# FFN output matrix by Strassen's scheme: 18 of 22 depth tiles, activation sums on VectorE, weight sums on GpSimd

## The reference, cut to what matters

```python
def swiglu(h, w_in, w_out):
    gate, up = jnp.split(h @ w_in, 2, axis=-1)
    return (jax.nn.silu(gate) * up) @ w_out
# per layer: D_MODEL = 1024, D_FF = 2816
x = x + 0.5 * swiglu(rms_norm(x, ffn1_norm[layer]), ffn1_w_in[layer], ffn1_w_out[layer])
x = x + mixer(rms_norm(x, mix_norm[layer]))
x = x + 0.5 * swiglu(rms_norm(x, ffn2_norm[layer]), ffn2_w_in[layer], ffn2_w_out[layer])
```

## Time and profile before

| | |
|---|---|
| median of 3 runs | 2288.98 us (2287.26 to 2289.0) |
| profiled execution, span from first to last instruction | 2285.9 us |
| median less that span | 3.1 us |
| TensorE busy | 2249.8 us (98%) |
| VectorE busy | 1633.5 us (71%) |
| ScalarE busy | 1049.8 us (46%) |
| GpSimd busy | 302.4 us (13%) |

### The profile page before, as it was taken

One profiled execution on the slowest core, in us unless ns is written; L12 is line 12 of the kernel. 1 busy time (PEld: TensorE's weight loads), 2 busy tenths in 40 slices (PEclk: granted clock), 3 DMA queues, 4 the chain that ended last, 5 costly groups with the idle time before them and its releaser, 6 DMA issues.

```text
span 2285.9 us, 45730 instructions
## 1 busy us (share of the span) xinstructions
PE 2249.8 (98%) x18915; PEld 2198.7 (96%) x18915; DVE 1633.5 (71%) x2712; ACT 1049.8 (46%) x1949; POOL 302.4 (13%) x257
## 2 busy tenths in 40 slices
PE   9999999999999999999999999999999999999998
PEld 8999999988989999999999999999988899999998
DVE  7876776557575977767877776689755657777674
ACT  5544444333323544444554444454444544444443
POOL 2100002000051100001200000144033632000001
PEclk9999999999999999999999999999999999999999
DMA  4222323322202233222222232322310012222321
GB/s 135 93 93 97 103 92 110 98 81 83 90 10 93 75 101 103 93 93 93 93 93 93 96 105 87 114 74 75 93 52 2 30 31 91 93 93 93 98 97 68
DMA packets 175052, 194.82 MB, mean 85 GB/s; under 512 B 4826, under 2 KB 155870, under 8 KB 174841
## 3 DMA queue, kind: packets, MB, share of 16 engines
q1 hardware_dynamic: 161902, 181.64, 24.3%
q10 hardware_dynamic: 12306, 8.18, 1.3%
q0 software_dynamic: 640, 2.10, 0.3%
HBM read 185.80 MB, written 6.10 MB: 84 GB/s over the span
## 4 chain that ended last, share of the span: by engine, by line
PE 85%; DVE 8%; ACT 2%; issue 2%; POOL 1%; DMA 1%; ACTq 0%; SPq 0%; DVEq 0%; POOLq 0%
PE ps L892 33%; PE ps L793 29%; PE ps L666 12%; DVE cacc L2419 2%; DVE wl L651 1%; PE ps L3320 1%; DVE pre L2408 1%; ACT cacc L2488 1%; DMA xnat<-x_prompt 1%; PE ps L1681 1%; PE ps L3165 0%; POOL dBl L2996 0%; PE ps L2152 0%; PE ps L3150 0%; PE ps L3200 0%
## 5 line engine op out<-in xcount | busy, mean ns | idle before, releaser
L892 PE MATMUL ps<-bop,wh 128*128 128x272 f32 x4032 | 761.0, 288 | 0.0
L892 PEld LDWEIGHTS ps<-bop,wh 128*128 128x128 f32 x4032 | 633.0, 188 | 0.0
L892 PE MATMUL ps<-bop,wl 128*128 128x272 f32 x2016 | 582.2, 289 | 0.0
L784 DVE TENSOR_TENSOR wl<-raw,wh 128x512 fp32r<-128x512 f32 (+1 forms) x456 | 317.5, 708 | 266.8 <-ACT wh L778 262.1
L892 PEld LDWEIGHTS ps<-bop,wl 128*128 128x128 f32 x2016 | 378.8, 188 | 0.0
L778 ACT ACTIVATE wh<-raw 128x512 fp32r<-128x512 f32 (+1 forms) x456 | 265.3, 611 | 217.2 <-PE ps L793 177.4
L793 PE MATMUL ps<-hl,wh 128*128 128x288 f32 (+1 forms) x1408 | 290.4, 287 | 0.0
L793 PE MATMUL ps<-hh,wl 128*128 128x288 f32 (+1 forms) x1408 | 289.5, 287 | 0.0
L793 PE MATMUL ps<-hh,wh 128*128 128x288 f32 (+1 forms) x1408 | 289.1, 286 | 0.0
L666 PE MATMUL ps<-xh,wh 128*128 128x288 f32 (+1 forms) x1056 | 224.7, 294 | 2.1 <-DVE wl L651 2.1
L778 ACT ACTIVATE wh<-wsum 128x512 fp32r<-128x512 f32 x256 | 159.6, 627 | 132.8 <-DVE wsum L1038 86.6
(11 more groups left out here) (490 smaller groups left out, 3586.5 us busy)
## 6 DMA issues: line engine op xcount, KB each, us to landing
raw<-ffn_w_in SPq DMA_DIRECT2D x88, 1024.0 KB, 5.0
raw<-ffn_w_out SPq DMA_DIRECT2D x32, 1024.0 KB, 5.1
raw<-odd_w_in SPq DMA_DIRECT2D x16, 1024.0 KB, 5.7
raw<-even_w_in SPq DMA_DIRECT2D x14, 1024.0 KB, 5.0
raw<-ffn_w_out SPq DMA_DIRECT2D x16, 768.0 KB, 4.2
raw<-even_w_out SPq DMA_DIRECT2D x4, 1024.0 KB, 5.0
raw<-odd_w_out SPq DMA_DIRECT2D x4, 1024.0 KB, 4.9
xnat<-x_prompt SPq DMA_DIRECT2D x2, 1024.0 KB, 11.9
```

The source lines that it names most:

```text
L784: nc.vector.tensor_tensor(lo[:, 0:nk, :], op_source(u, i), hi[:, 0:nk, :].bitcast(F32), ALU.subtract).then_inc(op_lo.sem, 1)
L892: ins = nc.tensor.matmul(ps[:, bank, 0:TH], w[:, k, :], bop[:, r, k, :], start=i in S_OPEN and k == 0 and a == 0, stop=k == KH - 1 and a = ...
```

## The change

The output matrix is multiplied by the same scheme over 18 of its 22 hidden tiles: three parts of three pairs of hidden tiles. A part has four "out" units, each with two output column tiles (256 columns) and six hidden tiles, seven blocks of 3 x 3 = 9 matmuls of 272 columns. They stand between the gate and the up unit of pairs 3, 6 and 9. The remaining four hidden tiles are multiplied plainly in two last units of four output columns each.
- The activations' blocks of a pair of hidden tiles (the two token halves of both tiles and four differences, `hidden_turns`) are made on VectorE during the unit after the pair's up unit, split by ScalarE and VectorE, and kept in `hop` (three pairs of buffers, which lie over `xh`, `xl` and the arena).
- The weight sums of all but the first two Strassen units, and those of the out units, are made by GpSimd (`block_sums_pool`).
- ScalarE copies four bank states of each out unit, at scale 0.5, into `comb`; VectorE adds them and two banks to `x` in five steps (`x_add` 1 to 4, and the fifth in `tail_dve`).

The core of the diff:

```diff
-MID_TILES = 4
-MID_PARTS = 4
+MID_PAIRS = 3
+MID_TILES = 2 * MID_PAIRS
+MID_PARTS = 3
 LAST_TILES = FT - MID_TILES * MID_PARTS
...
         for j in range(FJ):
-            for s in range(2):
-                add("whole" if j == 0 and s == 0 else "plain" if j < LEAD_PAIRS else "seven", j, s)
-            if LEAD_PAIRS <= j < LEAD_PAIRS + 2 * MID_PARTS:
-                add("mid", (j - LEAD_PAIRS) % 2, 0, (j - LEAD_PAIRS) // 2)
-        for q in range(4):
-            add("last", q, q % 2, MID_PARTS)
+            kind = "plain" if j < LEAD_PAIRS else "seven"
+            add("whole" if j == 0 else kind, j, 0)
+            if j and j % MID_PAIRS == 0:
+                for q in range(4):
+                    add("out", q, 0, j // MID_PAIRS - 1)
+            add(kind, j, 1)
+        for q in range(2):
+            add("last", q)
...
+    O_BANK = (4, 7, 4, 7, 4, 6, 4)
...
+    def early_block(u):
+        return u.block - first_block[u.f] < 2
...
-        if u.kind == "seven" and i in S_SUMS:
-            act.wait_ge(sum_made.sem, sum_made.at(4 * u.seven + S_SUMS[i] + 1))
+        if u.n_ops == 7 and i in S_SUMS:
+            sum_wait(act, u, S_SUMS[i] + 1)
...
+    def ffn_out_pe(pe, u):
+        f, p, q = u.f, u.part, u.pair
+        third = hidden_before(f, MID_PAIRS * (p + 1))
+        for i, o in enumerate(S_ORDER):
+            op = u.op + i
+            pe.wait_ge(op_lo.sem, op_lo.at(op + 1))
+            if q == 0 and i < 2:
+                pe.wait_ge(hl_ready.sem, hl_ready.at(third - (2 if i == 0 else 0)))
...
+            if i == 0 and u.out >= 2:
+                pe.wait_ge(x_part.sem, x_part.at(x_steps(u.out - 2, 5)))
+            elif i in (1, 5) and u.out >= 1:
+                pe.wait_ge(x_part.sem, x_part.at(x_steps(u.out - 1, 4)))
+            elif i in (2, 3, 4):
+                pe.wait_ge(bank_copied.sem, bank_copied.at(4 * u.block + i - 1))
+            elif i == 6:
+                pe.wait_ge(bank_copied.sem, bank_copied.at(4 * u.block + 4))
+            w_hi, w_lo = entry(op)
+            for k in range(MID_PAIRS):
+                for a, (w, r) in enumerate(((w_hi, 7 + o), (w_hi, o), (w_lo, 7 + o))):
+                    ins = nc.tensor.matmul(ps[:, block_bank(u, i), 0:TH], w[:, k, :], hop[k][:, r, :],
...
+    def hidden_turns(dve, u):
+        if not by_blocks(u):
+            return
+        f = hopf[u.pair % MID_PAIRS]
+        dve.wait_ge(h_made.sem, h_made.at(2 * FJ * u.f + 2 * u.pair + 2))
+        nc.vector.tensor_tensor(f[:, 3, :], sq[0][:, TH:T], sq[0][:, 0:TH], ALU.subtract).then_inc(turn_made.sem, 1)
+        nc.vector.tensor_tensor(f[:, 1, :], sq[1][:, TH:T], sq[0][:, TH:T], ALU.subtract).then_inc(turn_made.sem, 1)
+        dve.wait_ge(turn_made.sem, turn_made.at(turns_before(u) + 1))
+        nc.vector.tensor_tensor(f[:, 2, :], sq[1][:, TH:T], f[:, 3, :], ALU.subtract).then_inc(turn_made.sem, 1)
+        dve.wait_ge(turn_made.sem, turn_made.at(turns_before(u) + 3))
+        nc.vector.tensor_tensor(f[:, 0, :], sq[1][:, 0:TH], f[:, 2, :], ALU.subtract).then_inc(turn_made.sem, 1)
+
+    def hidden_lo(dve, u, step):
...
+            i, (at, n) = u.pair % MID_PAIRS, ((6, 1), (4, 2), (0, 4))[step]
+            src = (sq[0][:, 0:TH], two(sq[1][:]), hopf[i][:, 0:4, :])[step]
...
+    SUM_TERMS = (((1, 0), (1, 1), ALU.add), (None, (0, 0), ALU.subtract), ((0, 1), None, ALU.subtract), ((0, 0), (1, 0), ALU.subtract))
+
+    def block_sums_pool(pool, u):
+        slot, out, first = u.raw % 2, sums_of(u), ffns[u.f]
+        pool.wait_ge(raw_loaded[slot].sem, raw_loaded[slot].at(8 * (u.raw - slot) + 16))
+        if u.block - first_block[u.f] < 4:
+            pool.wait_ge(op_used.sem, op_used.at(first[3].op + 4))
+        else:
+            pool.wait_ge(op_lo.sem, op_lo.at(blocks[u.block - 2].op + 5))
+        for k, (a, b, alu) in enumerate(SUM_TERMS):
+            if a is None or b is None:
+                pool.wait_ge(sum_pool.sem, sum_pool.at(sums_before(u) + k))
+            left = out[:, k - 1, :, :] if a is None else block_raw(u, *a)
+            right = out[:, k - 1, :, :] if b is None else block_raw(u, *b)
+            nc.gpsimd.tensor_tensor(out[:, k, :, :], left, right, alu).then_inc(sum_pool.sem, 1)
...
-        if u.kind != "seven":
+        if u.n_ops != 7 or not early_block(u):
             return
...
+    def ffn_block_act(act, u):
...
+        next_split(act, op_split_hi, u, 0)
+        copy(0, M1C)
+        if hidden and regular:
+            hidden_hi(act, hidden, 0)
+        next_split(act, op_split_hi, u, 1)
+        copy(1, M5C)
+        if hidden and regular:
+            hidden_hi(act, hidden, 1)
+        next_split(act, op_split_hi, u, 2)
+        copy(2, U2C)
         next_split(act, op_split_hi, u, 3)
         late_act(act, ffns[u.f][u.at - 1])
...
+        if hidden and regular:
+            hidden_hi(act, hidden, 2)
         next_split(act, op_split_hi, u, 4)
+        copy(4, U3C)
...
+    def x_add(dve, u, step):
+        parts, m = comb[u.block % 2], 2 * u.pair
+        if step in (1, 3):
...
+            own = x[:, m + 1, TH:T]
+            nc.vector.tensor_tensor(own, own, parts[:, part, :], ALU.add).then_inc(x_part.sem, 1)
+        elif step == 2:
...
+            nc.vector.tensor_tensor(two(x[:, m, :]), two(x[:, m, :]), parts[:, M1C:U2C + 1, :], ALU.add).then_inc(x_part.sem, 1)
+        else:
...
+            nc.vector.scalar_tensor_tensor(out=two(x[:, m, :]), in0=ps[:, 6:8, 0:TH], scalar=0.5, in1=two(x[:, m, :]),
+                                           op0=ALU.mult, op1=ALU.add).then_inc(x_part.sem, 1)
...
+    def ffn_out_dve(dve, u):
+        next_split(dve, op_split_lo, u, 0)
+        tail_dve(dve, ffns[u.f][u.at - 1])
+        next_split(dve, op_split_lo, u, 1)
+        next_split(dve, op_split_lo, u, 2)
+        x_add(dve, u, 1)
+        next_split(dve, op_split_lo, u, 3)
+        x_add(dve, u, 2)
+        next_split(dve, op_split_lo, u, 4)
+        x_add(dve, u, 3)
+        next_split(dve, op_split_lo, u, 5)
+        x_add(dve, u, 4)
+        next_split(dve, op_split_lo, u, 6)
...
-            if u.kind == "mid":
+            if u.kind == "out":
                 k0 = MID_TILES * u.part
-                dst, src = wide_raw(slot), wo[:, k0:k0 + MID_TILES, 2 * UW * u.pair:2 * UW * (u.pair + 1)]
+                dst, src = raw[slot][:, 0:MID_TILES, :], wo[:, k0:k0 + MID_TILES, UW * u.pair:UW * (u.pair + 1)]
...
         ffn_lead_pool(pool, 0, 0)
+        ffn_sums_pool(pool, 0)
```

More of the change, by code:

```diff
@@ L594, in build @@
             u.op = op_count
-            u.n_ops = {"whole": 0, "plain": 4, "seven": 7, "mid": 4, "last": 4}[u.kind]
+            u.n_ops = {"whole": 0, "plain": 4, "seven": 7, "out": 7, "last": 4}[u.kind]
             if u.kind == "last":
-                ring_pos += -ring_pos % 4
+                ring_pos += -ring_pos % (RING if u.pair == 0 else 4)
             if u.kind == "seven":
@@ L600, in build @@
                 sevens.append(u)
+            if u.kind == "out":
+                u.out = len(outs)
+                outs.append(u)
+            if u.n_ops == 7:
+                u.block = len(blocks)
+                blocks.append(u)
             for i in range(u.n_ops):
                 e = ring_pos % RING
+                if u.kind == "last" and u.pair == 0:
+                    e = (i + 2) % 4
                 op_entry.append(e)
@@ L895, in ffn_seven_pe, with x_steps, hidden_before @@
             ins.then_inc(op_used.sem, 1)
[L897 to L904, removed]
+    def x_steps(out, step):
+        return X_STEPS * out + step
+    def hidden_before(f, pair):
+        whole = MID_PAIRS * MID_PARTS
+        return f * (3 * whole + 2 * (FJ - whole)) + 3 * min(pair, whole) + 2 * max(pair - whole, 0)
+    def ffn_out_pe(pe, u):
[3 more added lines that the diff above has]
+            op = u.op + i
@@ new lines, in build, with copy @@
+    M1C, U2C, M5C, U3C = range(4)
+    def ffn_block_act(act, u):
+        hidden = hidden_unit(u)
+        regular = u.at > 2 * LEAD_PAIRS + 1
+        def copy(op, out):
+            act.wait_ge(op_used.sem, op_used.at(u.op + op + 1))
+            if u.block >= 2:
+                last = blocks[u.block - 2]
+                if last.kind == "seven":
+                    act.wait_ge(block_out.sem, block_out.at(outs_before[last.seven + 1]))
+                else:
+                    act.wait_ge(x_part.sem, x_part.at(x_steps(last.out, 3)))
+            nc.scalar.activation(comb[u.block % 2][:, out, :], ps[:, block_bank(u, op), 0:TH], ACT.Copy,
+                                 scale=0.5 if u.kind == "out" else 1.0).then_inc(bank_copied.sem, 1)
@@ L1219, in ffn_seven_dve @@
     def ffn_seven_dve(dve, u):
-        before, pair, outs, side = ffns[u.f][u.at - 1], u.seven // 2, outs_before[u.seven], u.seven % 2
-        into = gbuf if u.s == 0 else sq
-        copied = lambda k: dve.wait_ge(bank_copied.sem, bank_copied.at(4 * u.seven + k))
```

(4 more changed lines are left out.)

405 lines of the change are left out of this document (221 added, 184 removed).

## The result

Time after: **2408.39 us**, median of 4 runs (2406.31 to 2413.58), against 2288.83 before (4 runs, 2287.26 to 2289.0): ratio 1.0527 (1.0513 to 1.0541), 119.6 us slower. The forecast had the sign (2335) but not the size; the time lies just over the end of its range (2405), and within 2 us of the "upper end" that its sum had named (327.0 us a stretch, 118 us lost). One of the four runs of experiment 6 took 2373.07 us at a mean clock of 0.849, where the other three had 0.995 or more, and is not counted.

The account below looks back on a forecast made before the run. TensorE's rate bounds the FFN, VectorE close behind. VectorE's work plus GpSimd's holds needs 291.0 to 327.0 us a stretch against 297.6; the middle loses 11.4 us an FFN, 46 in four: 2335 us, range 2240 to 2405.

Parts of the forecast that it names:

- upper end: Middle stretch: no GpSimd hold covered, 320.0 us plus about 7 us idle, 327.0; 118 us lost in four FFNs.
- TensorE's saving: FFN products: 948 instead of 1056 for the output matrix, 12.9 us an FFN, 51.5 us in four.
- VectorE's own work: Middle stretch: 180.1 us with both inputs in SBUF plus 29.0 with one in PSUM, 209.1 us an FFN.
- rival 1: FFN: TensorE stays the bound, GpSimd's sums fall into VectorE's gaps; 2237.5 us; chance 0.26, half of it in full.
- What a GpSimd sum costs VectorE: Middle stretch: each sum holds VectorE up 1.11 us (512 elements) or 0.83 (384), 110.9 us an FFN.
- a mean of 0.9 or more: Sign of being right: VectorE's residues of 128x512 grow from 0.69 us to this mean.
- I take the middle, 11.4 us lost: Per FFN, midway between 6.6 us gained (all PSUM instructions under GpSimd's) and 29.4 lost (none covered).
- the 7 us of the last unit: Stretch's last unit, where GpSimd has no sums left: about 7 of its 10.5 us idle, unusable.
- 8.3 to 9: Sign of being right: out units last this many us instead of 7.9.
- 11 to 12: Sign of being right: units last this many us instead of 10.5.
- 3 (GpSimd starved by 5 us a unit): VectorE's dense stretches: first Strassen unit of each of eight pairs loses 5 us, 160 us; 2450; chance 0.04.
- 4 (out units' second block waits for `x_add` step 4): Out units: a second GpSimd hold adds 0.83 us x 48 = 40 us on top; about 2375; chance 0.08.

Follow-up runs that it names:

- experiment 6: Changed kernel with GpSimd copying one block (one SBUF input) in place of each weight sum: 2249.07 us, ratio 0.9829.
- experiment 2: Changed kernel with GpSimd writing zeros in place of each weight sum, same waits, no SBUF reads: 2239.89 us, ratio 0.9788.
- experiment 1: Changed kernel with all weight sums back on VectorE, none on GpSimd: 2258.35 us, ratio 0.9871.
- experiment 8: Changed kernel with all weight sums on VectorE and the third activation split moved behind the last bank copy: 2257.89 us, ratio 0.9869.
- experiment 4: Changed kernel with GpSimd making only the Strassen input units' sums, VectorE the out units': 2350.16 us, ratio 1.0267.
- experiment 3: Changed kernel with GpSimd making only the out units' sums, VectorE the Strassen input units': 2323.91 us, ratio 1.0158.
- experiment 5: Kernel before, output matrix plain, with all Strassen units' sums except the first two units' of each FFN moved to GpSimd: 2297.54 us, ratio 1.0040.
- experiment 7: Changed kernel with 12 idle TensorE products added before the second block's wait in out units: 2435.98 us, ratio 1.0646.

## Why the sign was right and the size wrong

**TensorE's saving: right.** 284.7 forecast, 284.96 busy in experiment 2.

**VectorE's own work: right.** By the forecast's rates VectorE with all sums needs 209.1 + 64 x 0.60 + 48 x 0.47 = 270 us; experiment 1 has it busy for 277.2. The 7 us between them are put down here to the ends of instructions, which start-to-start rates leave out; no run separates them. (The prediction lets 68 weight sums leave VectorE; it is 64, and no sum of it uses the 68.) The time that it gave for sums left on VectorE, that of rival 1 (2237.5), was too low by 21 us, most of it in the first three units (experiment 8).

**What a GpSimd sum costs VectorE: right in total.** 310.1 busy after, less 209.1 and those 7, is 94 us for 112 sums, 0.84 us each; by experiment 2's 224.7 it is 85 us, 0.76 each. The forecast's middle had 110.9 less 14.5 that PSUM instructions cover: 96.4. Taken by halves in the same way, experiment 4 gives (299.4 - 231.7 - 7)/64 = 0.95 us for 512 elements and experiment 3 (286.9 - 247.5 - 7)/48 = 0.67 for 384, where the forecast had 1.11 and 0.83 before cover. (Where the prediction sets 0.60 against 1.11 us, 1.11 is its estimate of the hold; GpSimd itself starts a sum every 1.22 to 1.23 us.) That the exclusion is in reading SBUF, and not in the waits for GpSimd, experiments 1, 2, 5 and 6 show together. The residues, which were to show it ("a mean of 0.9 or more"), and GpSimd's sums:
```profile
L817 DVE TENSOR_TENSOR wl<-wsum,wh 128x512 fp32r<-128x512 f32 x256 | 230.7, 919 | 13.1 <-ACT wh L811 12.4
L817 DVE TENSOR_TENSOR wl<-wsum,wh 128x384 fp32r<-128x384 f32 x192 | 157.5, 829 | 21.5 <-ACT wh L811 20.9
...
L1150 POOL TENSOR_TENSOR wsum<-raw 128x512 f32<-128x512 f32 x128 | 214.4, 1678 | 321.0 <-DMA raw<-ffn_w_in 314.1 <-DVE wl L817 6.9
```
919 ns, against the 690 of experiment 2 (the residues of raw blocks of 512 elements have 873, against 717); and 1678 for a sum that takes 1270 undisturbed.

**The step that failed is "I take the middle, 11.4 us lost".** It halved two things at once: how much of GpSimd's holds PSUM instructions cover, which came out (96.4 us left uncovered by the forecast, 94 measured), and VectorE's idle time, which did not. It set VectorE busy for 209.1 + 96.4 = 305.5 us of 309.0, so that 3.5 us a stretch would be idle. Measured: 310.1 busy, 17.0 idle. Busy time is off by 4.6 us, less than the 7 us above; idle time by 13.5; together 18.1 a stretch, 72 of the 73 us that were missed. Halving the 7 us of the last unit was wrong in itself, for nothing can fill that place: VectorE is busy for 9.70 of the last 16.80 us of the second stretch. The other 10 us are a term that the prediction put at nothing: waits that an engine under full load meets in a ring with others. Before those last 16.8 us VectorE waited in the second stretch for ScalarE's high parts (`wh`):
```profile
DVE wl L817 <- ACT wh L811: 10.5, 14, 1.7
```
ScalarE's splits in turn waited there for TensorE to finish a block (32.3 us) and for GpSimd's sums (6.8 us), and they stand in one queue with the bank copies that TensorE waits for; which of these lies behind the 10.5 us was not separated. Experiments 3 and 4 have 19.0 and 15.1 us of idle VectorE too, experiment 5, where TensorE sets the pace, 69. So VectorE's busy time is a floor for the length of a stretch that no run reached. The upper end came out to 0.1 us, but by compensation: 320.0 + 7 forecast, 310.1 + 17.0 measured.

The sum over a whole stretch also hid where the time would go. The twelve out units of the second stretch, after and in experiment 2:
```profile
sum 116.04, PE 101.07 PEld 99.38 DVE 108.71 ACT 62.83 POOL 56.32; mean PE 33.69 PEld 33.13 DVE 36.24 ACT 20.94 POOL 18.77
sum 94.57, PE 94.57 PEld 94.57 DVE 73.25 ACT 62.96 POOL 21.42; mean PE 31.52 PEld 31.52 DVE 24.42 ACT 20.99 POOL 7.14
```
An out unit lasts 9.7 us, above the 8.3 to 9 that the prediction named as a sign; a Strassen unit 11.9, within its 11 to 12. Of the 44.3 us that the second stretch is longer than experiment 2's, 21.5 lie in the out units, a third of the stretch by TensorE's rate.

**The rivals.** 1 (sums hide in gaps) fell: VectorE's work and holds, 310 us, are above TensorE's 285; only when the sums hold up nobody, in experiment 2, is its time reached. 3 (GpSimd starved by 5 us a unit) did not come: by GpSimd's means (twice 1678 ns, 1524 and 1516) four sums of 512 elements take 6.4 us, within a unit. (Its 2450 adds its 160 us to the kernel before, not to the upper end that it names.) 4 (out units' second block waits for `x_add` step 4) came at its place, 41.4 us on L1374. That its price was 40 is luck, for there are 18 waits of 2.3 us where it had 48 of 0.83; and it did not come on top of the rest: with the out units' sums back on VectorE that wait is still there, 18.2 us in experiment 4, so it is partly where a VectorE that is late anyway meets TensorE.

**What stays open.** Four stretches are 4 x (327.1 - 285.5) = 166 us above experiment 2's. TensorE's listed waits are 118.6; 4 x (297.0 - 285.0) = 48 are TensorE taking longer over the same products. After some waits its granted clock falls to the lower of its two levels, 1.2 GHz, for some microseconds; the rows below (TensorE alone) show one wait of 2.31 us, for L1411, and 16 products in the 3 us from 931.00, 0.9 us after its end, instead of 26.
```profile
927.77:930.08 2.31, 0.00 (x0) 1.00 0.00 0
931.00:934.00 3.00, 3.00 (x16) 0.54 0.02 5
934.00:937.00 3.00, 3.00 (x24) 0.89 0.72 226
937.00:940.00 3.00, 3.00 (x26) 1.00 0.10 36
```
Whether those 48 us lengthen the kernel, or only fill time in which VectorE was late anyway, experiment 7 was to tell and did not. What starts the waits in the ring of VectorE, ScalarE and TensorE is open too.

## What to carry to other kernels

Price a move to a free engine by what it costs the engine it relieves: a sum of 512 elements that VectorE makes in 0.60 us held VectorE up for about 0.95 us when GpSimd made it. With slack such a move costs little (9 us in experiment 5), without slack everything (150 us here); so look first whether the freed engine was short at all, which the sum for experiment 1 could have said. When an engine's work plus holds comes out above the old bound, do not take its busy time for the length of the stretch: add the idle time that nothing can fill and that of the ring of waits. Here it was 15 to 19 us in stretches of 306 to 327; the forecast's own 305.5 us of busy time with that added would have given 320 to 325 us, for 327.1 measured. And make the sum by stages: half of the loss lay in the short out units, a third of the stretch.

## What the runs showed of the hardware that was not expected

- Beside GpSimd's writes of zeros a residue of 512 elements takes 690 ns on VectorE, and 685 with no GpSimd sums at all (experiments 2 and 1). A GpSimd instruction with one SBUF input still added 0.19 us to VectorE's busy time on average. The Trainium skill, "SBUF — State Buffer", section "Who interferes with whom", calls the shared port an exclusive lock; the trace agrees for two-input sums, while a copy (873 ns here for 512 elements) held VectorE up for less than its own length: a residue that met a copy of 0.71 us (at 866.85 in experiment 6) took 1.09 us instead of 0.68.
- The two engines meet in two ways within 8 us: at 914.99 GpSimd is kept waiting (2.76 us) while VectorE's instructions have their usual length, and from 917.84 they take turns, 1.4 to 1.5 us each.
- A wait of 2.31 us of TensorE was followed by a granted clock of 0.54 (931.00 to 934.00), and after its wait of 0.90 us, up to 924.50, the clock stayed at 1.00 (924.5 to 927.5).
